# First norm by input block, and the order of squares and weight splits in the last weight stage, of a hybrid decode step

## What is computed

```python
def rmsnorm(x, w):
    y = x * lax.rsqrt(jnp.mean(x * x, axis=-1, keepdims=True) + EPS)
    return y * w

p = rmsnorm(h, norm_mix) @ w_in          # q, k, v, gates, decays of both branches
...                                      # gated delta rule, stick-breaking attention, merge
def ffn_block(h, norm_w, w_in, w_out):
    gt, up = jnp.split(rmsnorm(h, norm_w) @ w_in, 2, axis=-1)
    return h + (silu(gt) * up) @ w_out
y = rmsnorm(hp, norm_final)
```

## Time and profile before

| | us |
|---|---|
| median of 3 runs | 1516.14 (1514.68 to 1516.35) |
| the profiled execution, its own time | 1516.05 |
| its span in the trace | 1514.3 |
| TensorE busy (matmul) | 1392.4 (92%) |
| VectorE busy | 808.5 (53%) |
| ScalarE busy | 513.6 (34%) |
| GpSimd busy | 194.5 (13%) |

### The profile page before, as it was taken

One profiled execution on the slowest core, in us unless ns is written; L12 is line 12 of the kernel. 1 busy time (PEld: TensorE's weight loads), 2 busy tenths in 40 slices (PEclk: granted clock), 3 DMA queues, 4 the chain that ended last, 5 costly groups with the idle time before them and its releaser, 6 DMA issues.

```text
span 1514.3 us, 28089 instructions
## 1 busy us (share of the span) xinstructions
PE 1392.4 (92%) x10686; PEld 1266.0 (84%) x10686; DVE 808.5 (53%) x2980; ACT 513.6 (34%) x780; POOL 194.5 (13%) x288
## 2 busy tenths in 40 slices
PE   5998989899999788888897999999999999989998
PEld 3997966678988788766675888898999999989998
DVE  4588739867889877753444421334544344332222
ACT  3432345637834332222124342223332223222112
POOL 1000002213220533301310000000111111110000
PEclk9999999999999879978898999999999999999999
DMA  9359946544541414439799999932333233322231
GB/s 318 106 183 320 294 147 204 174 151 137 169 107 44 153 36 121 131 89 329 243 344 319 350 341 317 308 127 70 95 87 98 84 98 93 89 81 77 77 91 68
DMA packets 254475, 252.58 MB, mean 167 GB/s; under 512 B 22433, under 2 KB 215083, under 8 KB 254309
## 3 DMA queue, kind: packets, MB, share of 16 engines
q1 hardware_dynamic: 254341, 250.79, 52.0%
HBM read 235.66 MB, written 15.29 MB: 166 GB/s over the span
## 4 chain that ended last, share of the span: by engine, by line
PE 71%; issue 8%; DVE 7%; DMA 5%; POOL 4%; ACT 3%; SPq 2%; POOLq 0%; ACTq 0%; DVEq 0%
PE ps L1051 55%; PE ps L1080 4%; DVE wring L2132 2%; DMA wring<-in_w_ffn_out 1%; PE ps L1353 1%; POOL R L2694 1%; PE ps L1469 1%; DMA kring<-in_cache_v 1%; DMA R<-in_state_rec 1%; PE ps L1092 1%; DVE kring L2132 1%; SPq L735 1%; PE ps L1034 1%; PE ps L1336 1%; PE ps L1292 1%
## 5 line engine op out<-in xcount | busy, mean ns | idle before, releaser
L1051 PE MATMUL ps<-obT_split,wring_split 128*128 128x268 f32 (+2 forms) x1296 | 265.7, 287 | 0.0
L1051 PE MATMUL ps<-obT_split,qv_split 128*128 128x260 f32 (+2 forms) x1040 | 220.4, 294 | 3.5 <-DVE wring_split L596 2.0
L1051 PEld LDWEIGHTS ps<-obT_split,wring_split 128*128 128x128 f32 (+1 forms) x1296 | 202.9, 190 | 0.6
L596 DVE TENSOR_TENSOR wring_split<-wring,vring_split 128x1024 fp32r<-128x1024 f32 (+1 forms) x92 | 118.1, 1284 | 155.7 <-ACT vring_split L590 155.4
L1051 PE MATMUL ps<-obT_split,vring_split 128*128 128x260 f32 (+1 forms) x960 | 197.3, 287 | 0.8 <-issue 0.8
L1051 PE MATMUL ps<-xn_split,vring_split 128*128 128x260 f32 (+1 forms) x960 | 193.7, 283 | 0.0
L1051 PEld LDWEIGHTS ps<-obT_split,qv_split 128*128 128x128 f32 (+1 forms) x1040 | 163.0, 191 | 30.4 <-issue 27.8
L1051 PE MATMUL ps<-xn_split,qv_split 128*128 128x260 f32 (+2 forms) x912 | 187.4, 287 | 0.0
L596 DVE TENSOR_TENSOR wring_split<-wring,qv_split 128x1024 fp32r<-128x1024 f32 (+1 forms) x73 | 90.9, 1246 | 149.3 <-ACT qv_split L590 149.2
L1051 PEld LDWEIGHTS ps<-obT_split,vring_split 128*128 128x128 f32 x960 | 148.5, 189 | 3.0 <-issue 2.6
L1051 PEld LDWEIGHTS ps<-xn_split,vring_split 128*128 128x128 f32 x960 | 148.4, 189 | 0.1
(11 more groups left out here) (400 smaller groups left out, 2223.2 us busy)
## 6 DMA issues: line engine op xcount, KB each, us to landing
wring<-in_w_in SPq DMA_DIRECT2D x72, 512.0 KB, 5.4
kring<-in_cache_k SPq DMA_DIRECT2D x64, 512.0 KB, 5.0
vring<-in_cache_v SPq DMA_DIRECT2D x64, 512.0 KB, 5.7
kring<-in_cache_v SPq DMA_DIRECT2D x64, 512.0 KB, 5.5
wring<-in_w_ffn_in SPq DMA_DIRECT2D x44, 512.0 KB, 3.8
vring<-in_cache_k SPq DMA_DIRECT2D x24, 512.0 KB, 5.1
R<-in_cache_k SPq DMA_DIRECT2D x24, 512.0 KB, 7.2
wring<-in_cache_k SPq DMA_DIRECT2D x16, 512.0 KB, 4.5
```

Source lines behind the costliest of these rows:

```text
L596: nc.vector.tensor_tensor(fr(w_part(wlo[:, p % RING, :], p)), w_part(wring[:, p % RING, :], p), w_part(w_high(p), p), ALU.subtract).then_i ...
L1051: last = mm(ps[0:m, 2 * (t % 2) + i, 0:n], fr(w), fr(x[k][:, a + i * n:a + i * n + n]), start=(k == 0 and w is w_h and x is hi), stop=(k = ...
```

## The change

In the first stage: the last block of x is loaded first, and blocks 1, 2 and 3 by a load each; each block has a semaphore (two semaphore arrays of the middle are merged to make room). ScalarE takes the roots of each block as its sum arrives and scales it; VectorE scales block 3 only. The 24 last rows are transposed ahead of all else into bank 7, scaled by the norm's weights by VectorE and split in three instructions for all eight k. The eight rounds of x take four PSUM banks in turn. The splits of the first two weight tiles are moved in between the rounds. The 24 transposes of the convolution states and the copies of their results are moved behind the first weight tile. In the last weight stage: the one wait for all of h's low parts becomes a wait per block in the first tile, and ScalarE squares tile n before it splits tile n+2. The rest counts semaphores anew.

```diff
+X_ORDER = (4, 0, 1, 2, 3)
+RT_INPUT = 2 * TT
...
             def load_x():
+                sp.dma_start(xs0[0:LASTP, 4, :], io["x_prompt"][4 * P - META:SEQ, :]).then_inc(x_in[4], 16)
+                sp.dma_start(xs0[LASTP:LAST, 4, :], io["x_sample"]).then_inc(x_in[4], 16)
                 sp.dma_start(xs0[0:META, 0, :], io["meta_tokens"]).then_inc(x_in[0], 16)
                 sp.dma_start(xs0[META:P, 0, :], io["x_prompt"][0:P - META, :]).then_inc(x_in[0], 16)
-                sp.dma_start(xs0[:, 1:4, :], io["x_prompt"][P - META:4 * P - META, :]
-                             .rearrange("(t p) d -> p t d", p=P)).then_inc(x_in[1], 16)
...
+                for t in (1, 2, 3):
+                    sp.dma_start(xs0[:, t, :], io["x_prompt"][t * P - META:t * P - META + P, :]).then_inc(x_in[t], 16)
...
+            def transpose_tail():
+
+                pe.wait_ge(xs_ready, 1)
+                for k in range(KT):
+                    m = tr(ps[:, 7, LAST * k:LAST * k + LAST], xs0[0:LAST, 4, k * P:k * P + P], ident[0:LAST, 0:LAST])
+                m.then_inc(xt_tail, 1)
+
             def transpose_x0():
 
                 pe.wait_ge(xs_ready, TT)
                 for k in range(KT):
-                    if k >= 2:
-                        pe.wait_ge(g_hi, k - 1)
-                        pe.wait_ge(g_lo, k - 1)
-                    b = 2 + 2 * (k % 2)
+                    if k >= 4:
+                        pe.wait_ge(g_hi, k - 3)
+                        pe.wait_ge(g_lo, k - 3)
                     for t in range(4):
-                        tr(ps[:, b, t * P:t * P + P], xs0[:, t, k * P:k * P + P], ident[:, :])
-                    tr(ps[:, b + 1, 0:LAST], xs0[0:LAST, 4, k * P:k * P + P], ident[0:LAST, 0:LAST])\
-                        .then_inc(xt_ready, 1)
+                        m = tr(ps[:, 2 + k % 4, t * P:t * P + P], xs0[:, t, k * P:k * P + P], ident[:, :])
+                    m.then_inc(xt_ready, 1)
...
             pe.wait_ge(const_ready, CONSTS)
+            transpose_tail()
             pe.wait_ge(par_in, 16 * 8)
...
-            pe.wait_ge(par_c, 2)
-            pe.wait_ge(cst_in, 16)
-            for n in range(NQKV):
-                m = tr(ps[:, 6 + n // 12, 24 * (n % 12):24 * (n % 12) + 24], cst[0:24, n * P:n * P + P],
-                       ident[0:24, 0:24])
-            m.then_inc(par_t, 1)
             transpose_x0()
...
+            pe.wait_ge(xt_tail, 4)
             for t in range(T_SEG):
                 tile_split(t, n_hi, n_lo, None if t else 0, first_token(t), g_lo)
+                if t == 0:
+                    conv_states()
...
-            pe.wait_ge(a_lo, 2 * KT + FT)
             for n in range(KT):
-                tile_split(T_FO + n, h_hi, h_lo)
+                tile_split(T_FO + n, h_hi, h_lo, None if n else 2 * KT)
...
+            def input_scale(i, t):
+
+                n = rows_of(t)
+                ss, rs = tok_ss[0:n, t:t + 1], tok_rs[0:n, t:t + 1]
+                act.wait_ge(ms_ready, 2 + i)
+                go(rs, ss, ACT.Ln, scale=1.0 / D, bias=epsc[0:n, :]).then_inc(rt_ready, 1)
+                act.wait_ge(rt_ready, 2 * i + 1)
+                go(rs, rs, ACT.Exp, scale=-0.5).then_inc(rt_ready, 1)
+                if t != 3:
+                    act.wait_ge(rt_ready, 2 * i + 2)
+                    go(xs0[0:n, t, :], xs0[0:n, t, :], ACT.Copy, scale=rs).then_inc(xs_ready, 1)
...
-            split_hi(act, 0)
-            act.wait_ge(ms_ready, 1 + TT)
-            inverse_roots(0, [(tok_rs, tok_ss)])
-            act.wait_ge(rt_ready, 2)
-            for t in (3, 4):
-                n = rows_of(t)
-                go(xs0[0:n, t, :], xs0[0:n, t, :], ACT.Copy, scale=tok_rs[0:n, t:t + 1]).then_inc(xs_ready, 1)
-            split_hi(act, 1)
+            for i, t in enumerate(X_ORDER):
+                input_scale(i, t)
             act.wait_ge(par_c, 1)
             for k in range(KT):
                 act.wait_ge(xt_ready, k + 1)
...
+                go(fr(n_hi[k][:, 0:512]), ps[:, 2 + k % 4, :], ACT.Copy, scale=cols[:, k:k + 1]).then_inc(g_hi, 1)
+                if k == 0:
+                    act.wait_ge(xt_tail, 2)
+                    go(fr(obT2[:, :, 512:TOKENS]), tail, ACT.Copy).then_inc(xt_tail, 1)
+                if k == 2:
+                    split_hi(act, 0)
+                if k == 5:
+                    split_hi(act, 1)
...
             for n in range(KT):
+                square(KT + n, sq2, READ_COUNT[T_FO + n])
                 if n + 2 < KT:
                     split_hi(act, T_FO + n + 2)
-                square(KT + n, sq2, READ_COUNT[T_FO + n])
...
+            for t in X_ORDER:
+                dve.wait_ge(x_in[t], 32 if t in (0, 4) else 16)
                 token_sums(t)
+            dve.wait_ge(rt_ready, RT_INPUT)
+            v.tensor_scalar(xs0[:, 3, :], xs0[:, 3, :], tok_rs[:, 3:4], None, ALU.mult).then_inc(xs_ready, 1)
...
+            dve.wait_ge(xt_tail, 1)
+            v.tensor_tensor(tail, ps[:, 7, 0:LAST * KT].rearrange("p (k t) -> p k t", k=KT),
+                            per_head(cols[:, 0:KT], LAST), ALU.mult).then_inc(xt_tail, 1)
             for k in range(KT):
...
+                if k == 0:
+                    dve.wait_ge(xt_tail, 3)
+                    v.tensor_tensor(fr(xn2[:, :, 512:TOKENS]), tail, obT2[:, :, 512:TOKENS], ALU.subtract).then_inc(xt_tail, 1)
+                if k == 3:
+                    split_lo(dve, 0)
+                if k == 6:
+                    split_lo(dve, 1)
```

More of the change, by code:

```diff
@@ L496, in build @@
         dsm = sb("dsm", [P, 10, 64])
+        tail = dsm[:, 0:3, :].rearrange("p a b -> p (a b)").rearrange("p (k t) -> p k t", k=KT)
         krow, vrow = rows[64:P, 0:P], rows[64:P, P:2 * P]
@@ L512, in build @@
         const_step, const_ready, selv_ready = sem("const_step"), sem("const_ready"), sem("selv_ready")
-        x_in = [sem("x_in0"), sem("x_in1")]
+        x_in = [sem(f"x_in{i}") for i in range(TT)]
+        xt_tail = sem("xt_tail")
         par_in, pt_in, cst_in = sem("par_in"), sem("pt_in"), sem("cst_in")
@@ L544, in build @@
         tu_zero, u4_in = sem("tu_zero"), sem("u4_in")
-        tu_in = [sem(f"tu_in{i}") for i in range(4)]
+        inv_state_in = [sem(f"inv_state_in{i}") for i in range(4)]
         n_sq, n_ss, n_act, n_dve, n_tt = (sem(n) for n in ("n_sq", "n_ss", "n_act", "n_dve", "n_tt"))
@@ L550, in build @@
         g_pe, g_act, g_dve, g_pool = (sem(n) for n in ("g_pe", "g_act", "g_dve", "g_pool"))
-        t_in = [sem(f"t_in{i}") for i in range(4)]
         t_pe, t_dve, t_act, t_pool = (sem(n) for n in ("t_pe", "t_dve", "t_act", "t_pool"))
@@ L1316, in levels @@
                     if LEVELS[c]:
-                        pe.wait_ge(tu_in[c], 128)
+                        pe.wait_ge(inv_state_in[c], 128)
                     for s in LEVELS[c]:
@@ L1434, in sampled_step @@
                     for q in range(4):
-                        pe.wait_ge(t_in[q], 16)
+                        pe.wait_ge(inv_state_in[q], 128 + 16)
                         if q >= 2:
@@ L1476, in _, with conv_states @@
             tr(ps[:, 6, P:P + 96], crow[0:96, :], ident[0:96, 0:96]).then_inc(par_t, 1)
-            pe.wait_ge(par_c, 2)
-            pe.wait_ge(cst_in, 16)
-            for n in range(NQKV):
-                m = tr(ps[:, 6 + n // 12, 24 * (n % 12):24 * (n % 12) + 24], cst[0:24, n * P:n * P + P],
-                       ident[0:24, 0:24])
-            m.then_inc(par_t, 1)
-            transpose_x0()
+            transpose_x0()
+            def conv_states():
+                pe.wait_ge(par_c, 2)
+                pe.wait_ge(xt_tail, 2)
+                pe.wait_ge(cst_in, 16)
+                for n in range(NQKV):
+                    m = tr(ps[:, 6 + n // 12, 24 * (n % 12):24 * (n % 12) + 24], cst[0:24, n * P:n * P + P],
+                           ident[0:24, 0:24])
+                m.then_inc(par_t, 1)
             def spread_head(h):
@@ L1632, in inverse_roots @@
                 m.then_inc(rt_ready, 1)
-                act.wait_ge(rt_ready, 2 * u + 1)
+                act.wait_ge(rt_ready, RT_INPUT + 2 * (u - 1) + 1)
                 for dst, src in pairs:
@@ L2093, in _ @@
             for n in range(KT):
+                square(KT + n, sq2, READ_COUNT[T_FO + n])
                 if n + 2 < KT:
                     split_hi(act, T_FO + n + 2)
-                square(KT + n, sq2, READ_COUNT[T_FO + n])
             act.wait_ge(ms_ready, 1 + TT + 2)
             inverse_roots(2, [(tok_rs[:, 0:4], tok_ss[:, 0:4]), (tok_rs[0:DB, 4:5], tok_ss[0:DB, 4:5])])
-            act.wait_ge(rt_ready, 6)
+            act.wait_ge(rt_ready, RT_INPUT + 4)
             for t in range(TT):
@@ L2499, in _ @@
             dve.wait_ge(ms_ready, 1)
-            dve.wait_ge(x_in[0], 16 * 4)
-            token_sums(0)
-            token_sums(4)
-            dve.wait_ge(x_in[1], 16)
-            for t in (1, 2, 3):
+            for t in X_ORDER:
+                dve.wait_ge(x_in[t], 32 if t in (0, 4) else 16)
```

(6 more changed lines are left out.)

29 lines of the change are left out of this document (6 added, 23 removed).

## The result

The changed kernel takes **1490.57 us** (median of 4 runs, 1488.77 to 1493.57) beside 1515.41 (4 runs, 1514.01 to 1516.35) for the kernel before on the same chip: a ratio of 0.9839, 95% interval 0.9819 to 0.9859. The profiled execution took 1491.81 us with a span of 1490.1, beside 1516.05 and 1514.3.

A forecast was written before the change was run, and what follows sets the result against it. The prediction took the kernel to be bound by a chain of waits, 71% of it TensorE working. From 1516.05 us it took 12.2 for the last stage and 5.3 for the first: 1498.5, range 1495 to 1503.

The forecast's parts named there:

- TensorE works at 1.2 GHz until real matmuls have run for a while: First stage: transposes don't raise the clock, so the rounds stay at 1.04 us each.
- 8 x 1.04 = 8.3 us: First stage: eight rounds of x's transposes at 1.04 us each, so the first tile starts at 22.3 instead of 31.44.
- 1.1 for the clock: First stage: a loss of 0.8 us for a possible fall behind the 24 small transposes and 0.3 for a later rise.
- Rival 2: First stage: transposes get the fast clock, saving 1.4 us in the rounds and 0.8 to 1.1 after: 1496; chance 0.08.
- (a): Last stage, first tile: with a wait per block of h, TensorE goes on 4.2 us earlier.
- (b): Last stage, first tile: with only 0.7 us of standing still the clock doesn't fall, saving 1.6 us.
- (c): Last stage: with the square ahead of the split, six of TensorE's seven waits for it go, saving 4.8 us.
- (d): Last stage: the fall of the clock after the 2.0 us wait goes, saving 1.6 us.
- The pipeline: First stage: ScalarE takes 1.66 us a block, the last scaling ends at 13.45, and TensorE starts on x at 14.0.
- Rival 1: The middle takes the first stage's gain back, or clock and parameters both end badly: 1500.3 to 1503.9; chance 0.2.
- Rival 3: SyncE's stop ahead of key page 14 makes the last pages late and TensorE stands: 1517 and up; chance 0.02.
- Rival 4: A wait for weights holds the last stage's first tile, so 5.8 us of gain are lost: 1504.3; chance 0.03.

The follow-up runs named there:

- e4: The changed kernel with both edits of the last weight stage undone: 1505.78 us, ratio 0.9930 to the kernel before.
- e8: The changed kernel, but VectorE waits for all five blocks of x before its first sum: 1496.19 us, ratio 0.9873 to the kernel before.
- e9: The changed kernel with 14 unused identity transposes on TensorE ahead of its wait for the parameters: 1491.03 us, ratio 0.9828 to the kernel before.
- e10: The changed kernel with the eight parameter loads issued from ScalarE's queue and its table load ahead of its wait for the constants: 1492.66 us, ratio 0.9842.
- e6: The changed kernel with the 24 transposes of the convolution states back ahead of the rounds: 1495.60 us, ratio 0.9868 to the kernel before.
- e5: The changed kernel with two PSUM banks in turn for the rounds of transposes instead of four: 1497.95 us, ratio 0.9877 to the kernel before.
- e7: The kernel before with a third pair of PSUM banks for the rounds, each keeping its small transpose: 1513.45 us, ratio 0.9984.
- e11: The changed kernel with one small transpose of the 24 last rows added to each round, into an unread bank: 1496.81 us, ratio 0.9867.
- e2: The kernel before with only the wait for all of h made a wait per block in the last stage: 1510.02 us, ratio 0.9956.
- e3: The kernel before with both edits of the last weight stage and nothing of the first: 1501.27 us, ratio 0.9897.
- e1: The kernel before with only ScalarE's square of tile n put ahead of the split of tile n+2: 1508.35 us, ratio 0.9946.

## Why the prediction was wrong, point by point

- **The step that failed** is "TensorE works at 1.2 GHz until real matmuls have run for a while". It was read from 32 transposes that never got faster, and those stood in a pattern that the change takes apart: a small transpose after every four large ones, and waits for banks. Four large ones back to back, round after round, rose after three to four rounds (after, e4, e8, e9, e10), in e6 after six and a half. e5 holds them down with waits alone, e7 and e11 with the small ones alone. The other reason was a rule of the Trainium skill ("TensorE: Matmul & The Clock Gate", Part 4: PE-mode transpose), that full clock does not engage for transposes. The trace of the changed kernel differs (272 ns, and a first tile that starts with short pairs), so the measurement decides; e5, e7 and e11 each show a pattern in which it looks true.
- **A second step was mis-sized** and has nothing to do with the clock: the term 8 x 1.04 = 8.3 us for the rounds. The 1.04 holds the handover to the small transpose, which the change takes out. Large ones alone take 0.85 us a round at the slow pace: 6.9.
- What the two were worth, up to the second tile: the terms of the prediction make 32.8 (22.3, then 6.7 for the first tile as before, 2.7 for the transposes behind it and 1.1 for the clock), and it started at 27.6. The rounds took 5.7 us and not 8.3: 1.4 of that is the mis-sized term, 1.2 the rise. The rise also spared the first tile its slow pairs (6.1 us for 6.7, 0.6) and let the charge of 1.1 for the clock fall away (there is no fall behind the 24 small transposes: from its second pair on the second tile takes 0.40 a pair). The 24 small transposes took 1.6 us and not 2.7 (213 to 237 ns each for 276), 1.1. Less 0.3 for the start at 14.26 instead of 14.0, that is 5.1 of the 5.2 us, 4.0 of it by the clock.
- **Rival 2** named this cause, and gave it 0.08 and 1496. Its mechanism was right; its size was off. It counted from 1.04 a round, and let VectorE's 0.7 us bound a round, though four banks give slack: after the rise there were two short stops, 0.1 and 0.4 us between starts. And it left out that the 24 small transposes would be fast and that no fall would follow them.
- **The last stage**: (a) 4.2, (b) 1.6, (c) 4.8 and (d) 1.6 hold within 0.3 us as far as rows show them (waits of 0.9 and 0.3 left, so (a) gave 3.9; 15.8 us a tile, 1.00 in every window). A term was missing: the sums of the squares behind a TensorE that hasn't stood add 0.91 us and not 1.18, 6 x 0.27 = 1.6. From the first matmul to the end of the last tile it was 133.8 us (1342.55 to 1476.32), where 135.2 was said. That the whole stage gave only 12.6 and not 13.8 is the 0.3 of (a), 0.2 within the tiles, and 0.7 behind the last tile (13.8 us to the end of the span for 13.1 before), a stretch that takes 12.0 to 13.8 in the profiles here.
- The pipeline: ScalarE's pace came as said (1.6 us a block against 1.66), but it began 1.0 us late behind its table load, which had been put at its old time, and the last scaling ended at 14.20 for 13.45. The parameters landed at 13.36, in the bounds of 12.7 and 13.6, and their transposes were done at 14.01. So the scaling and not the parameters set the start of the rounds. That 14.26 lies so near the 14.0 of the prediction is in part luck.
- **Rival 1** fell: the middle gave nothing back (1315.1 before, 1314.0 after). **Rival 3** fell: the pages' first use is at 46.2, where 47 was said, and from 32 to 110 us TensorE waits 1.0 us in all (0.6 before), for ScalarE's reads alone. **Rival 4** fell with e2 and e3.
- The forecast of the sum was 7.3 us short by medians and 6.7 by the two profiles: 5.3 in the first stage (10.6 in place of 5.3), 0.4 in the last, 1.1 in the middle. The 1.1 us of the middle are less than its differences between the profiles of other kernels here (1311.3 in e1, 1317.5 in e2), and stay open.

## What to carry to other kernels

A duration read from the trace of before is a property of the instruction in its surroundings. Where a change alters what stands between instructions (waits, small ones in the mix), price the clock-bound ones at both levels, and give the faster level a chance that doesn't rest on the old pattern. Take the price from start to start of like instructions: a stretch that ends at another kind holds the handover to it. Two causes that were removed together have to be put back one at a time: here either alone, the waits or the small transposes, cost 5 to 6 us again, about half of it by the clock. And a change of many edits is worth splitting by stations: the starts and ends of four tiles on TensorE told that the last stage was near and the first wasn't. The same care holds for experiments: e10 moved the small loads and, by that, the weights too, so its loss has two possible causes.

## What the hardware showed that was not expected

- Transposes of 128 x 128 in f32, back to back, went from 421 ns to 272 ns within the same unbroken series; the 24 x 24 ones from 276 to 213. A 24 x 24 transpose after every four large ones kept all of them slow for ten microseconds without a gap (e7, e11).
- After a standing TensorE the ten square sums add 1.18 us to the chain, straight behind a tile 0.91 (1.07 from first start to last end), at a granted clock of 1.00 in both (1412.70 to 1414.00 before, 1374.40 to 1375.40 after).
- A fall of the clock in the same place cost 1.6 us in one execution and 2.8 in another (before, e1), behind waits of 4.8 and 5.1 us: one price for it, taken from one profile, is uncertain by that much. The same code of the whole last stage, from its first matmul to the end of its last tile, took 143.2 us before, 144.6 in e7 and 146.1 in e4.
- With eight small loads issued early on ScalarE's queue and the weights issued 3.1 us earlier on SyncE's, the last of the small loads landed a microsecond later than in the changed kernel, and the last block of x 2.9 us later (e10).
